# Residual additions moved to VectorE, and squares summed by TensorE, at the seams of a two-block transformer kernel

## What is computed

```python
def first_block(x, ...):
    h = rmsnorm(x, pre_mix_g) * (1.0 + sc1) + sh1
    y = hybrid_mixer(h, ...)                 # attention, convolution, gates, y = merged @ w_o
    x = x + ga1 * rmsnorm(y, post_mix_g)     # seam A: add, then norm again
    h = rmsnorm(x, pre_ffn_g) * (1.0 + sc2) + sh2
    y = swiglu_ffn(h, w_ffn_in, w_ffn_out)
    x = x + ga2 * rmsnorm(y, post_ffn_g)     # seam B: add, then the next block's norm
    return x

def second_block(x, ...):
    h = rms_norm(x, attn_norm_w)
    proj = h @ w_in                          # retention q, k, v, gate; latents
    ...
    x = x + mixed @ w_out
    x = x + conv_ffn(rms_norm(x, ffn_norm_w), w_up, conv_w, conv_b, w_down)
    return rms_norm(x, final_norm_w)         # C: the end
```

## Time and profile before

| | |
|---|---|
| times of the three runs, us | 1559.96, 1561.6, 3719.56 (median 1561.6) |
| span of the profiled execution, us | 1559.9 |
| PE busy | 1415.3 us, 91%, 6318 instructions |
| DVE busy | 901.2 us, 58%, 1101 instructions |
| ACT busy | 639.0 us, 41%, 820 instructions |
| POOL busy | 123.9 us, 8%, 87 instructions |
| chain that ended last | PE 35% of the span, DVE 3%, ACT 2% (the part that could be followed) |

### The profile page before, as it was taken

One profiled execution on the slowest core, in us unless ns is written; L12 is line 12 of the kernel. 1 busy time (PEld: TensorE's weight loads), 2 busy tenths in 40 slices (PEclk: granted clock), 3 DMA queues, 4 the chain that ended last, 5 costly groups with the idle time before them and its releaser, 6 DMA issues. The chain is left out here.

```text
span 1559.9 us, 16871 instructions
## 1 busy us (share of the span) xinstructions
PE 1415.3 (91%) x6318; PEld 1147.9 (74%) x6318; DVE 901.2 (58%) x1101; ACT 639.0 (41%) x820; POOL 123.9 (8%) x87
## 2 busy tenths in 40 slices
PE   5998999989687799999995989867899999999996
PEld 3788888767366678888883788646787888888884
DVE  4798888667743233332337647477655754673663
ACT  3323666653433122222224644456635522341432
POOL 0000000002300091000016000000010000000002
PEclk9999999999899999999997999986899999999998
DMA  9431111136222432322220210020023232323221
GB/s 366 168 139 62 54 54 40 67 126 263 110 81 81 154 109 81 108 101 88 89 98 36 98 65 32 11 75 34 0 81 109 81 108 81 108 81 108 81 66 69
DMA packets 27415, 146.71 MB, mean 94 GB/s; under 512 B 3169, under 2 KB 4193, under 8 KB 14945
## 3 DMA queue, kind: packets, MB, share of 16 engines
q1 hardware_dynamic: 27360, 145.99, 26.1%
HBM read 143.88 MB, written 2.10 MB: 94 GB/s over the span
## 5 line engine op out<-in xcount | busy, mean ns | idle before, releaser
L1199 DVE TENSOR_TENSOR w_lo<-raw,w_hi 128x2048 fp32r<-128x2048 f32 (+4 forms) x120 | 251.4, 2095 | 185.3 <-ACT w_hi L687 182.1
L687 ACT ACTIVATE w_hi<-raw 128x2048 fp32r<-128x2048 f32 (+4 forms) x115 | 197.8, 1720 | 163.0 <-PE psum L414 84.4
L414 PE MATMUL psum<-h_hi,w_hi 128*128 128x512 f32 x736 | 191.8, 403 | 22.6 <-DVE w_lo L1199 22.6
L414 PE MATMUL psum<-h_hi,w_lo 128*128 128x512 f32 x736 | 183.9, 391 | 0.0
L414 PE MATMUL psum<-h_lo,w_hi 128*128 128x512 f32 x736 | 182.8, 389 | 0.0
L414 PEld LDWEIGHTS psum<-h_hi,w_hi 128*128 128x128 f32 x736 | 140.8, 194 | 55.1 <-issue 22.3
L414 PEld LDWEIGHTS psum<-h_lo,w_hi 128*128 128x128 f32 x736 | 138.2, 188 | 28.7
L414 PEld LDWEIGHTS psum<-h_hi,w_lo 128*128 128x128 f32 x736 | 138.0, 188 | 29.0 <-issue 0.5
L1814 POOL COPY sq_sum<-sq 128x512 f32<-128x512 f32 x6 | 5.5, 921 | 1200.1 <-ACT sq L731 1200.1
L414 PE MATMUL psum<-xg_hi,w_lo 128*128 128x512 f32 x336 | 85.3, 396 | 0.0
L414 PE MATMUL psum<-xg_lo,w_hi 128*128 128x512 f32 x336 | 85.3, 396 | 0.0
(11 more groups left out here) (312 smaller groups left out, 2335.6 us busy)
## 6 DMA issues: line engine op xcount, KB each, us to landing
raw<-w_ffn_in SPq DMA_DIRECT2D x22, 1024.0 KB, 4.7
raw<-w_up SPq DMA_DIRECT2D x22, 1024.0 KB, 4.7
ada_first<-ada SPq DMA_DIRECT2D x16, 512.0 KB, 10.0
raw<-w_gate SPq DMA_DIRECT2D x8, 1024.0 KB, 4.7
raw<-w_mix_out SPq DMA_DIRECT2D x8, 1024.0 KB, 4.8
raw<-w_ffn_out SPq DMA_DIRECT2D x8, 1024.0 KB, 4.7
raw<-w_down SPq DMA_DIRECT2D x8, 1024.0 KB, 4.7
ada_mid<-ada SPq DMA_DIRECT2D x11, 512.0 KB, 6.2
```

The lines of the kernel that those rows point to most:

```text
L414: last = mm(ps, w[slot][:, k, t * P:(t + 1) * P], xv[:, k0 + k, :], start=first, stop=final)
L687: A(w_hi[slot][:, 0:stage.kc, :], raw[slot][:, 0:stage.kc, :], ACT.Copy).then_inc(sem["w_hi_done"], 1)
L1199: return tt(out_lo, full, high.bitcast(F32), ALU.subtract)
```

## The change

Odd chunks of both residual additions move from POOL to DVE: in `add_normed` DVE now adds chunk c-1 after it has made t_n for chunk c, for every c, and h_lo follows one chunk at a time, three behind. attn2 leaves the norms that POOL sums; its eight ones products stand behind the six matmuls of each chunk in `first_group`. For post_mix, post_ffn and final POOL sums six squares, and PE multiplies that sum and the last two squares, in one accumulation (`stat_sum_and_last`). conv_ln and ffn2 stay as they were; the guard of sq_sum changes its semaphore.

```diff
--- before.py
+++ after.py
@@ -86,7 +86,10 @@
     NORMS[_name] = (_e, _q, _n)
     _q += _n
 
-ADDED_NORMS = ["conv_ln", "post_mix", "post_ffn", "attn2", "ffn2", "final"]
+ADDED_NORMS = ["conv_ln", "ffn2"]
+LAST_BY_PE = {"post_mix": 2, "post_ffn": 2, "final": 2}
+SUM_READ = {"post_mix": ("stat_done", 1), "post_ffn": ("sum_done", "post_mix"), "ffn2": ("sum_done", "post_ffn"),
+            "final": ("stat_done", 2)}
 
 MADE = {"pre_mix": 0, "conv": 8, "pre_ffn": 12, "attn2": 20, "lat": 28, "gn": 31, "ffn2": 35}
 
@@ -385,12 +388,23 @@
                 o_ps_read(name)
                 mm(o_ps, ones[:, :], sq_sum[:, :], start=True, stop=True).then_inc(sem["stat_done"], 1)
 
-            def stat_chunks(name, into=o_ps):
+            def stat_sum_and_last(name):
 
                 e, q0, n = NORMS[name]
-                if into is o_ps:
+                q1 = q0 + n - LAST_BY_PE[name]
+                pe.wait_ge(sem["sum_done"], q1)
+                o_ps_read(name)
+                mm(o_ps, ones[:, :], sq_sum[:, :], start=True, stop=False)
+                for q in range(q1, q0 + n):
+                    pe.wait_ge(sem["sq_done"], q + 1)
+                    mm(o_ps, ones[:, :], sq[q % 2][:, :], start=False, stop=(q == q0 + n - 1)).then_inc(sem["sum_done"], 1)
+
+            def stat_chunks(name, into=o_ps, chunks=None):
+
+                e, q0, n = NORMS[name]
+                if into is o_ps and not chunks:
                     o_ps_read(name)
-                for c in range(n):
+                for c in chunks or range(n):
                     pe.wait_ge(sem["sq_done"], q0 + c + 1)
                     mm(into, ones[:, :], sq[(q0 + c) % 2][:, :], start=(c == 0), stop=(c == n - 1)).then_inc(sem["sum_done"], 1)
 
@@ -415,7 +429,7 @@
                 if passes[-1] == PASSES - 1:
                     last.then_inc(sem["tile_done"], 1)
 
-            def first_group(stage, x_hi, x_lo, k0, ready, beside=None):
+            def first_group(stage, x_hi, x_lo, k0, ready, beside=None, after=None):
 
                 for k in range(stage.kc):
                     if beside and k == 3:
@@ -428,6 +442,8 @@
                                       start=(n == 0 and k == 0), stop=(n == 2 and k == stage.kc - 1))
                         if k == stage.kc - 1:
                             last.then_inc(sem["tile_done"], 1)
+                    if after:
+                        after(k)
 
             def weights(g):
                 pe.wait_ge(sem["w_lo_done"], g + 1)
@@ -550,20 +566,20 @@
             gemm(st["att_out"], h_hi, h_lo, k0=4, steps=(1, 2))
             gemm(st["conv_out"], h_hi, h_lo, ready=("made_lo", MADE["conv"], 0))
             gemm(st["mix_out"], mid_hi, mid_lo, ready=("mid_lo_done", 0, 0))
-            stat_sum("post_mix")
+            stat_sum_and_last("post_mix")
             stat_chunks("pre_ffn")
             for r, n in enumerate(FFN_PARTS):
                 gemm(st[f"ffn_in{r}"], h_hi, h_lo, ready=("made_lo", MADE["pre_ffn"], 0) if r == 0 else None)
                 gemm(st[f"ffn_out{r}"], mid_hi, mid_lo, ready=("mid_lo_done", 8 + PART_AT[r], 0))
-            stat_sum("post_ffn")
+            stat_sum_and_last("post_ffn")
 
             weights(st["ret_qk"].g0)
-            first_group(st["ret_qk"], h_hi, h_lo, 0, ("made_lo", MADE["attn2"], 0))
+            o_ps_read("attn2")
+            first_group(st["ret_qk"], h_hi, h_lo, 0, ("made_lo", MADE["attn2"], 0),
+                        after=lambda k: stat_chunks("attn2", chunks=[k]))
             weights(st["ret_qk"].g0 + 1)
-            tile(st["ret_qk"], 1, 0, h_hi, h_lo, passes=range(1))
-            stat_sum("attn2")
-            tile(st["ret_qk"], 1, 0, h_hi, h_lo, passes=range(1, PASSES))
-            tile(st["ret_qk"], 1, 1, h_hi, h_lo)
+            for t in range(2):
+                tile(st["ret_qk"], 1, t, h_hi, h_lo)
             gemm(st["ret_qk"], h_hi, h_lo, steps=(1, 2))
             gemm(st["ret_val"], h_hi, h_lo, rows=True)
 
@@ -665,7 +681,7 @@
                 else:
                     gemm(st[f"up{r}"], xg_hi, xg_lo)
                 gemm(st[f"down{r}"], mid_hi, mid_lo, ready=("mid_lo_done", 8 + FC + PART_AT[r], 0))
-            stat_sum("final")
+            stat_sum_and_last("final")
 
 
         @block.scalar
@@ -1467,12 +1483,12 @@
                         if c >= 2:
                             dve.wait_ge(sem["x_odd" if c % 2 else "x_even"], first // 2 + c // 2)
                         stt(t_n[c % 2][:, :], y[:, c, :], gain[:, g, c:c + 1], rs[:, :], ALU.mult, ALU.mult).then_inc(sem["upd_step"], 1)
-                    if c % 2:
+                    if c:
+                        b = c - 1
                         dve.wait_ge(sem["upd_step"], first + c)
-                        tt(x[:, c - 1, :], x[:, c - 1, :], t_n[0][:, :], ALU.add).then_inc(sem["x_even"], 1)
-                        if low and c > 1:
-                            low(c - 3)
-                            low(c - 2)
+                        tt(x[:, b, :], x[:, b, :], t_n[b % 2][:, :], ALU.add).then_inc(sem["x_odd" if b % 2 else "x_even"], 1)
+                    if low and c >= 3:
+                        low(c - 3)
                 dve.wait_ge(sem["x_even"], first // 2 + DC // 2)
                 dve.wait_ge(sem["x_odd"], first // 2 + DC // 2)
 
@@ -1801,16 +1817,15 @@
         def _(pool):
             tt, ts = nc.gpsimd.tensor_tensor, nc.gpsimd.tensor_scalar
 
-            def sums(name, ahead=None):
+            def sums(name):
 
                 e, q0, n = NORMS[name]
-                for q in range(q0, q0 + n):
-                    if ahead:
-                        ahead(q - q0)
+                for q in range(q0, q0 + n - LAST_BY_PE.get(name, 0)):
                     pool.wait_ge(sem["sq_done"], q + 1)
                     if q == q0:
-                        if ADDED_NORMS.index(name):
-                            pool.wait_ge(sem["stat_done"], ADDED_NORMS.index(name))
+                        if name in SUM_READ:
+                            by, at_least = SUM_READ[name]
+                            pool.wait_ge(sem[by], at_least if by == "stat_done" else sum(NORMS[at_least][1:]))
                         last = nc.gpsimd.tensor_copy(sq_sum[:, :], sq[q % 2][:, :])
                     else:
                         pool.wait_ge(sem["sum_done"], q)
@@ -1819,14 +1834,6 @@
 
             for name in ["conv_ln", "post_mix"]:
                 sums(name)
-
-            def add_odd(first, c):
-
-                pool.wait_ge(sem["upd_step"], first + c + 1)
-                tt(x[:, c, :], x[:, c, :], t_n[1][:, :], ALU.add).then_inc(sem["x_odd"], 1)
-
-            for c in range(1, DC, 2):
-                add_odd(0, c)
 
             steps = [0]
 
@@ -1851,9 +1858,7 @@
                 step(tt(turns[:, :], turns[:, :], angle[:, :], ALU.subtract))
                 ts(cos_t[:, :], turns[:, :], -1.0, float(np.float32(np.pi / 2)), ALU.mult, ALU.add).then_inc(sem["ang_arg"], 1)
 
-            sums("post_ffn")
-            sums("attn2", lambda c: add_odd(DC, 1 if c == 0 else c + 2) if c == 0 or c % 2 and c < DC - 2 else None)
-            for name in ["ffn2", "final"]:
+            for name in ["post_ffn", "ffn2", "final"]:
                 sums(name)
```

## The result

The changed kernel takes 1549.98 us (median of four runs, 1547.64 to 1551.57) against 1561.38 for the kernel before, measured beside it. The ratio is 0.9917 with a 95% interval of 0.9902 to 0.9932: 13.0 us, with an interval of 10.6 to 15.3. The two medians alone stand 11.4 us apart (0.9927). The ratio on record, which the interval belongs to, isn't their quotient; it leaves out one execution of the kernel before that took 3719.56 us. The prediction was 1550.4 and 11.2, inside the interval.

The account below looks back on a forecast made before the run. PE was busy 91% of the span, so time could be won only where it stands still or runs at the lower clock. Gains of 2.9 + 5.4 + 2.9 = 11.2 us from 1561.6 gave 1550.4 us, range 1549 to 1553.

Parts of the forecast that it names:

- A, before the adds: Mixer-to-feed-forward seam: ada columns return to 1.28, DVE decides the start of the additions, near 407; gain 2.0 us.
- A, the adds: Mixer-to-feed-forward seam: each chunk costs DVE 1.40 us, Ln of pre_ffn comes at 420.0; seam's gain 2.9 us.
- It moves as a whole: ffn_in0, behind the mixer-to-feed-forward seam: a chain of its own weight waits, so the seam's 2.9 us passes through.
- A's gain is lost: Rival at the mixer-to-feed-forward seam: clock stays low for pre_ffn's eight products, seam loses 1.5, total 1555 us; chance 0.15.
- B, up to the first chunk: Feed-forward-to-retention seam: Ln 2.9 us earlier, first h_lo 5.6 us after the adds start, PE begins at 836.9 to 837.0.
- B, the first group: ret_qk's first group: pitch 2.4 us, 5 us of lower clock, 21.6 us in all, PE the bound; seam's gain 5.4.
- more at B: Rival at ret_qk's first group: clock rises after 4 us, pitch 2.29, gain 6.7, total 1549 us; chance 0.15.
- Before, DVE set it: ret_qk's first group in the kernel before: DVE was taken to set its 21.0 us, from 841.29 to 862.31.
- The reason given for B: Feed-forward-to-retention seam: POOL's work taken as the cause of h_lo's 1.75 us; every h_lo should fall to 0.75.
- C: End of the kernel, final norm: last product directly behind the last tile, Ln at 1547.45 instead of 1550.37; gain 2.9 us.
- Slow clock: Rival at ret_qk's first group: short waits keep PE's clock low throughout, 36.8 us, total about 1565; chance 0.07.
- Sum: Whole kernel: gains at the two seams and the end, 2.9 + 5.4 + 2.9 = 11.2 us, giving 1550.4 us.

Follow-up runs that it names:

- A alone: Kernel before with only the mixer-to-feed-forward seam changed (all additions on DVE, post_mix's last two squares on PE): 1558.62 us, ratio 0.9975.
- C alone: Kernel before with only the end changed (PE takes the final norm's last two squares): 1559.38 us, ratio 0.9976.
- r_clock_kept: Changed kernel plus matmuls nobody reads in PE's pauses at the first seam, in ffn_in0, before ffn_out0 and before ret_qk: 1546.69 us, ratio 0.9897.
- r_last_two_only: Kernel before with only the last two squares of post_mix, post_ffn and final moved to PE: 1554.68 us, ratio 0.9946.
- r_B_pool_sums: Changed kernel, but POOL sums attn2's squares again, with the ones product back in the second group: 1551.05 us, ratio 0.9930.
- r_B_pool_adds: Changed kernel, but POOL adds the odd chunks again at the feed-forward-to-retention seam, with h_lo in pairs: 1554.14 us, ratio 0.9947.
- the change again: The changed kernel itself, unaltered, run once more for a second profile and a tighter ratio: 1550.16 us, ratio 0.9920.
- B alone: Kernel before with only the feed-forward-to-retention seam changed (additions on DVE, post_ffn's last two squares and attn2's squares on PE): 1554.62 us, ratio 0.9947.
- r_B_last_two_only: Changed kernel, but POOL has odd additions and attn2's squares again at the feed-forward-to-retention seam: 45.48 us from ffn_out2's last tile to ret_qk's third group.

## Why the prediction was right, point by point

- **A, before the adds:** the ada columns at 1.28, the start at 406.99 against 407.06, gain 2.07 against 2.0. Exp began at 405.74, so rs was ready at 406.4 and not at 405.8: ACT's table load, which the sum had left out here, held Ln until 405.02. DVE still decided, as said, but by 0.6 us and not by 1.3.
- **A, the adds:** pitch 1.39 against 1.40, Ln 2.81 earlier against 2.9. The backlog of PE was gone by the fifth product.
- **"It moves as a whole":** not borne out. The whole time of A alone agrees with it (3.9, from 2.2 to 5.6), but in the traces only about half of the gain is left at ffn_out0, and in the trace of A alone none of it at the end of ffn_out2. In a single execution the clock of the first group and the landing of the weights moved the end by up to 3.6 us. How much of A's 2.8 passes stays open. The rival *A's gain is lost* had the wrong place: pre_ffn's products did get the full clock.
- **B, up to the first chunk:** Ln 3.75 earlier on the span's clock, of which 0.91 came from A: 2.84 against 2.9. The first chunk at 836.02 stands 10.51 behind the last tile, where the prediction had 10.5 to 10.6.
- **B, the first group:** in this profile two terms came out smaller. The pitch was 2.31, not 2.4: it alternates between 2.2 and 2.4 to 2.5. The lower clock lasted 3.3 us, not 5, but that was luck: over four executions it was 3.3 to 6.0, 4.8 on average, as forecast. The group and the wait behind it took 21.0 us (836.02 to 857.03) where the prediction had 22.5 (837 to 859.4). The third group came 42.54 behind the last tile, where the prediction had 43.9; its wait and the product of 0.9 were gone, as said. Gain 6.8 in this profile, like the rival *more at B* (6.7), and 5.7 between the means, near the forecast of 5.4.
- **"Before, DVE set it":** true up to the last h_lo, which ends at 858.87. The rest of the old group was PE's lower clock, up to 860: with a shorter second spell A alone's old group and the wait behind it take 19.9 us (841.21 to 861.06) instead of 21.0. The prediction read this spell only for how long it lasts, and gave it no price.
- **The reason given for B was only half right.** POOL did stretch h_lo, since all are at 0.74 to 0.76 without it. But undoing POOL's sums costs about 1 us, not the 4 to 6 that I expected from this reason. The prediction itself had the reason in another sentence: PE becomes the bound at 2.29 per chunk. A bound of 2.3 on PE leaves little of a DVE that gets faster than that. About half of B (2.8 of 5.7) came with the shorter chain of the last two products alone.
- **C:** 2.83 against 2.9 in this pair, 2.3 against the mean of three old ones. The sum took over the product of 2.1 us on the fallen clock from the one profile; in two others it took 1.2 and 1.5.
- **Slow clock:** no sign of it; with waits of 0 to 0.1 us between chunks the clock stayed at 1.00 to the group's end.
- **Sum:** B gave 1.4 more in the profile, A 2.0 less up to ffn_out0, and 2.1 came between 868 and 1534, in stages that I had taken to move as a whole. The traces settle this last one. From ret_qk's third group to the last addition it is 668.0 to 668.6 us in four traces (before, C alone, r_clock_kept, r_last_two_only) and 666.2 to 666.8 in the nine others, A alone among them, which changes nothing from B on. Between before and after, 1.2 of the 2.1 is a spell at the lower clock behind the wait at 926.16 (918.22 after), 5.2 us against 2.9, and 1.1 is another behind the wait at 1120.41 (1111.65 after). It is chance, not the change. The near hit of the total (11.2 against 12.7) rests partly on luck: errors that made up for one another, and spells at the lower clock that were long in the one profile and short in the other.

## What to carry to other kernels

The chain that ends a sum over chunks is worth shortening first: adding the last two squares on the engine that must do the product anyway gave about two thirds of this change (8.4 of 12.5 us) for twelve matmul instructions. Before moving work between VectorE and GpSimd to undo a stretch, ask which engine would be the bound without the stretch; here TensorE took over at nearly the same pitch. When a sum of waits is checked against one profile, look at the same stretch in other executions, where the edit does nothing, before a difference of 1 or 2 us is given a cause. And when a stage waits for weights in every group, read what stands ahead of the load in its queue before touching any engine: two transfers exchanged in every round gave twice as much as all the rest.

## What the runs showed of the hardware

- TensorE's spell at the lower clock in the same first group at B lasted 3.3 us (after), 5.1 (before), 5.7 (r_B_pool_sums) and 6.0 (r_B_pool_adds, and the change again), behind pauses of 7.1 to 8.6 us; at A it was 3.0 (before) and 5.6 (after), behind 4.02 both times. A sum that contains such a spell is uncertain by some 2.6 us at half speed, 1.3 us of work.
- The same float32 product behind the same pause of 4.19 us at C took 1.17, 1.48 or 2.08 us, by where the clock fell (A alone, B alone, before).
- Two waits of 1.37 and 1.35 us, 3.0 us apart (r_B_pool_sums), did not lower the clock. A wait of 2.96 to 3.00 us at the same place of B lowered it in four executions (before, A alone, C alone, r_B_last_two_only) and not in a fifth (r_last_two_only).
- The weights' transfers of ffn_in0, all of one size, took 5.2 to 8.0 us from issue to use, and the sum over six differed by 3 us between executions (37.9 before, 41.0 in A alone).
- A 0.68 us addition on DVE took 1.76 beside a POOL addition, and POOL's 1.33 became 1.66; each waited for the other to finish.
